# Down projections of a SwiGLU block: two 256-column products joined into one of 512 columns

## The reference, cut to what matters

```python
D_MODEL, SEQ, DEC_SEQ, D_FF = 1024, 512, 32, 2816
def swiglu(x, w_gu, w_down):
    gate, up = jnp.split(x @ w_gu, 2, axis=-1)
    return (jax.nn.silu(gate) * up) @ w_down

h = h + 0.5 * swiglu(rms_norm(h, p['norm_ffn1'][l]), p['ffn1_w_gu'][l], p['ffn1_w_down'][l])
```

## Time and profile before

| | us |
|---|---|
| median of 3 runs | 2352.0 |
| lowest, highest | 2350.32, 2352.34 |
| the profiled execution, its own time | 2351.26 |
| its span, first to last instruction | 2349.6 |
| PE busy | 2300.7 |
| DVE busy | 1721.3 |
| ACT busy | 1138.6 |

### The profile page before, as it was taken

The page is one execution under the profiler, slowest core; times in us unless marked ns, Lnnn a source line. Parts: engine busy times, 40 slices in busy tenths (PEclk is TensorE's granted clock), DMA queues, the critical chain, the costliest instruction groups (busy, mean ns, idle before and its releaser), DMA issues.

```text
span 2349.6 us, 49786 instructions
## 1 busy us (share of the span) xinstructions
PE 2300.7 (98%) x20579; PEld 2264.5 (96%) x20579; DVE 1721.3 (73%) x2569; ACT 1138.6 (48%) x1743; POOL 13.3 (1%) x50
## 2 busy tenths in 40 slices
PE   8999999999999999999999999999999999999998
PEld 8999999998999999999999999999999989999997
DVE  7767876788577567686867767876888867767875
ACT  6434444576355445343435434444677755434442
POOL 1000000000000000000000000000000000000000
PEclk9999999999999999999999999999999999999999
DMA  4333333332422233333333333332222223323331
GB/s 147 85 95 101 91 97 86 93 118 74 120 71 70 68 90 90 91 97 102 91 87 93 90 90 102 91 97 82 73 75 61 67 73 94 95 83 101 97 91 57
DMA packets 397772, 209.91 MB, mean 89 GB/s; under 512 B 11679, under 2 KB 393750, under 8 KB 397558
## 3 DMA queue, kind: packets, MB, share of 16 engines
q1 hardware_dynamic: 392166, 203.17, 30.4%
q10 hardware_dynamic: 5392, 3.72, 0.5%
HBM read 201.41 MB, written 5.45 MB: 88 GB/s over the span
## 4 chain that ended last, share of the span: by engine, by line
PE 71%; DVE 12%; ACT 6%; DVEq 6%; issue 3%; ACTq 1%; DMA 0%; SPq 0%
PE PM L2501 7%; PE PM L2503 7%; PE PM L2502 7%; PE PD L2417 7%; PE PD L2422 6%; PE PD L2423 6%; PE PD L2421 6%; PE PD L2418 6%; PE PD L2424 6%; PE PD L2503 3%; PE PD L2501 3%; PE PD L2502 3%; DVE wlo L1426 2%; ACT whi L619 1%; DVEq L1572 1%
## 5 line engine op out<-in xcount | busy, mean ns | idle before, releaser
L619 ACT ACTIVATE whi<-raw 128x1024 fp32r<-128x1024 f32 (+3 forms) x236 | 234.3, 993 | 362.4 <-PE PD L2424 356.4
L1426 DVE TENSOR_TENSOR wlo<-raw,whi 128x1024 fp32r<-128x1024 f32 (+3 forms) x238 | 273.5, 1149 | 87.1 <-ACT whi L619 65.3
L2417 PE MATMUL PD<-XB,whi 128*128 128x288 f32 x856 | 262.4, 307 | 4.8 <-DVE wlo L1426 4.5
L2422 PE MATMUL PD<-XB,whi 128*128 128x288 f32 x856 | 252.2, 295 | 0.0
L2423 PE MATMUL PD<-XB,wlo 128*128 128x288 f32 x856 | 252.0, 294 | 0.0
L2421 PE MATMUL PD<-XB,whi 128*128 128x256 f32 x856 | 241.2, 282 | 0.3 <-DVE XB L1464 0.3
L2418 PE MATMUL PD<-XB,whi 128*128 128x256 f32 x856 | 239.7, 280 | 0.0
L2424 PE MATMUL PD<-XB,wlo 128*128 128x256 f32 x856 | 237.5, 278 | 0.0
L2417 PE MATMUL PD<-AB,whi 128*128 128x288 f32 x704 | 209.8, 298 | 5.6 <-ACT AB L722 4.6
L2501 PE MATMUL PM<-XT,WH 128*128 128x272 f32 x720 | 208.3, 289 | 4.7 <-ACT PM L698 3.3
L2503 PE MATMUL PM<-XT,WL 128*128 128x272 f32 x720 | 208.2, 289 | 0.0
(11 more groups left out here) (500 smaller groups left out, 6590.1 us busy)
## 6 DMA issues: line engine op xcount, KB each, us to landing
raw<-in_ffn_w_down SPq DMA_DIRECT2D x64, 512.0 KB, 3.8
V<-in_ffn_w_gu SPq DMA_DIRECT2D x60, 512.0 KB, 4.0
V<-in_ffn_w_gu SPq DMA_DIRECT2D x120, 256.0 KB, 4.5
raw<-in_ab_w_in SPq DMA_DIRECT2D x44, 512.0 KB, 3.9
raw<-in_ffn_w_gu SPq DMA_DIRECT2D x32, 512.0 KB, 3.9
raw<-in_c_w_in SPq DMA_DIRECT2D x32, 512.0 KB, 4.1
raw<-in_ffn_w_down SPq DMA_DIRECT2D x32, 384.0 KB, 3.3
VF<-in_ffn_w_gu SPq DMA_DIRECT2D x12, 512.0 KB, 4.8
```

Source lines behind the costliest of these rows:

```text
L619: A(whi[ps % 2][:, 0:k, :], raw[ps % 4][:, 0:k, :], ACT.Copy).then_inc(S["hi_ready"], 1)
L1426: TT(wlo[u % 2][:, 0:k, :], raw[u % 4][:, 0:k, :], whi[u % 2][:, 0:k, :].bitcast(F), ALU.subtract).then_inc(S["lo_ready"], 1)
L2417: mm(front, hi, x[:, 0, r, 0:FRONT], start=first, stop=False)
L2422: mm(front, hi, x[:, 1, r, 0:FRONT], start=False, stop=False)
```

## The change

For a unit of a block's first two groups (`joined`, 64 units), the two products of the high weights by the rear tokens, one with high and one with low x, become one matmul of 512 columns: the moving operand is a view of both halves of x, and the result fills the whole rear bank (`rests`), sum of high in the first 256 columns and of low in the next. The other four matmuls are as they were; the one with the low weights adds to the first 256 columns. The wait for the low part of x stands ahead of the merged matmul. When the unit is read, DVE multiplies the second 256 columns into the scratch tile UR, before the line is released, and adds them to H in a second step. Units of the third group and all other units are unchanged.

```diff
+        def rests(b):
+
+            at0 = 1024 * (b % 2) + 512
+            return PDF[:, at0:at0 + 2 * REST].rearrange("p (s t) -> p s t", s=2)
+
+        def joined(u):
+
+            return any(plan[f"{tag}_down{g}"][0] <= u < plan[f"{tag}_down{g}"][0] + KT for tag, _ in FFNS for g in range(len(GROUPS) - 1))
...
             def scaled_residual(m, ps):
 
                 TT(RT[:, :], line(ps), RS[:, :], ALU.mult)
+                if joined(ps):
+                    TT(UR[:, 0:REST], rests(ps)[:, 1, :], RS[:, FRONT:T], ALU.mult)
                 dve.drain().then_inc(S["pair_read"], 1)
                 STT(H[:, m, :], RT[:, :], 0.5, H[:, m, :], ALU.mult, ALU.add)
                 dve.drain()
+                if joined(ps):
+                    STT(H[:, m, FRONT:T], UR[:, 0:REST], 0.5, H[:, m, FRONT:T], ALU.mult, ALU.add)
+                    dve.drain()
...
                 mm(front, hi, x[:, 0, r, 0:FRONT], start=first, stop=False)
-                mm(rest, hi, x[:, 0, r, FRONT:T], start=first, stop=False)
-                if before:
-                    before(1)
-                mm(rest, hi, x[:, 1, r, FRONT:T], start=False, stop=False)
+                if joined(ps):
+                    if before:
+                        before(1)
+                    mm(rests(ps), hi, x[:, :, r, FRONT:T], start=first, stop=False)
+                else:
+                    mm(rest, hi, x[:, 0, r, FRONT:T], start=first, stop=False)
+                    if before:
+                        before(1)
+                    mm(rest, hi, x[:, 1, r, FRONT:T], start=False, stop=False)
```

## The result

The changed kernel takes 2365.48 us in the median (2362.57 to 2365.91, 5 runs) against 2352.0 before: a ratio of 1.0052, 95% interval 1.0037 to 1.0067. Slower by 13.5 us between the medians (12.2 by the ratio), where 4 were forecast and 2361.5 was the upper end. The profiled execution took 2365.91, its span is 2364.2.

A forecast was written before the change was run, and what follows sets the result against it. PE was taken as the bound, with DVE close behind. Six-row groups +5.8, their late exit +1.0, eight-row groups -2.6 and first rows -0.2 gave +4.0 us: 2356.0, 0.17% slower, range 2350.0 to 2361.5.

The forecast's parts named there:

- The merged matmul, 0.225 us: PE, joined rows: 512 columns take 0.225 us start to start against the pair's 0.236, gaining 0.0116 us a row.
- the gain of 2.6 in eight-row groups: PE, eight-row groups: seven units of each group count, saving 2.6 us over the four FFNs.
- the two paces: PE: rows run at 0.747 or 0.753 us without a nameable cause, scattering the forecast by 2 us.
- proportional 512: Rival, chance 0.22: merged matmul on PE costs 0.236 or more, saving nothing; +7.7 us, 2359.7.
- cheap 512: Rival, chance 0.13: merged matmul on PE takes 0.215, saving 0.021 a row; +1.3 us, 2353.3.
- The merged wait, taken at 0: PE, group's last hidden row: waiting for x's low part hides under the existing bubble; 0, upper bound 0.9 us.
- DVE's added time, 0.84: DVE, each joined unit: product 0.34 plus second addition 0.50, together 0.84 us, 54 us over all.
- The chain: DVE, six-row groups: late reads delay the low weights, so PE waits at units 5, 6 and 7.
- the recurrence: Step-by-step DVE read times in the six-row group from unit 2: group longer by 1.54 us, later FFNs +1.37.
- the dear matmul: Merged matmul at 0.236 instead of 0.225: six-row group +1.75 a FFN, exit 0.18.
- The exit, 0.25 behind the group's end: After each six-row group: line 1548 on DVE comes 0.25 late and PE pays it, +1.0 us in all.
- The eight-row groups hide it: DVE, eight-row groups: 1.17 us idle less 0.84 and 0.09 leaves 0.2, so the added work is hidden.

The follow-up runs named there:

- dve_only: Kernel before, six matmuls a row, with only DVE's two added 256-column operations in the 64 units: 2361.47 us, ratio 1.0039.
- filled_joined: Changed kernel with unread 272-column matmuls put into PE's wait at each group's last hidden row: 2360.46 us, ratio 1.0041 to the kernel before.
- early_next_joined: Changed kernel with the next down unit's first rows put ahead of the group's last hidden row on PE: 2355.01 us, ratio 1.0018 to the kernel before.
- second_only: Kernel before with the change in the six-row groups alone (32 units): 2360.61 us, ratio 1.0047.
- first_only: Kernel before with the change in the eight-row groups alone (32 units): 2351.84 us, ratio 1.0000.

## Why the prediction was wrong, by its steps

*The merged matmul, 0.225 us.* This step failed: the term was sized too small. I had two readings of the excess over the columns' own time, fixed per matmul or growing with them, and took the fixed one for the reason that both rows near by showed "about that excess". The rows spoke for the other: 0.016 for 32 columns where 0.013 are the columns. Measured 0.234 in place, 0.232 in a plain stream. Of the gain of 2.6 in eight-row groups nothing came, but for the 0.4 that stems from the two paces. The rival "proportional 512" was the case: +7.7, 3.7 more than the forecast's sum; "cheap 512", 0.215, was not.

*The merged wait, taken at 0.* This step failed too, and its upper bound held: 0.10 for each of eight groups. The bubble behind the wait was not covered by the longer matmul but added to it: 0.34 to the next start, where the matmul takes 0.234 without a wait.

*DVE's added time, 0.84.* Right: 0.82. *The chain* was right in its mechanism: PE's starts of units 5, 6 and 7 from that of unit 2 were computed at 13.43, 18.47 and 23.97, and are 13.48, 18.49 and 23.97 in the first block (units of 4.49, 4.49, 4.50, 5.01, 5.48). At unit 5 the match is a coincidence: the forecast had it wait for 0.2 behind units of 4.41, and it does not wait, since three units of 4.49 take as long; units 6 and 7 wait as computed. From the start of unit 1 to the end of unit 7 the group takes 33.06 us where it took 31.36, so it lost 1.70, where the recurrence gave 1.54, or 1.75 with the dear matmul.

*The exit, 0.25 behind the group's end.* With the dear matmul it was computed at 0.18. It cost 0.13 in the first and 0.12 in the fourth block, and 0.47 and 0.48 in the middle two. There DVE stands idle once for a part that the profile puts down to nothing but "issue", 0.49 ahead of line 1524 in the third block (0.14 in the others), and in the second:

```profile
1125.12 1.76 DVE L1551 TENSOR_TENSOR WL<-V,WH 128x1536 fp32r<-128x1536 f32 x1 [0.43 <-issue]
```

The same two idle times stand in dve_only, filled_joined and early_next_joined, and not in second_only, whose six-row groups have the same edit. Why is open.

*The eight-row groups hide it.* Right for these groups by themselves, shown by first_only.

*What the sum did not hold* is the clock. No step asked what PE's pause at the last hidden row does to it; it stood at nothing without a reason, and the scatter that I allowed was for the two paces of the rows. Three falls cost 4.6 us in the profiled execution. That the pause has a part in them is supported by filled_joined and early_next_joined; why the merged form tips it and the six-matmul form, whose pause is 0.1 us shorter, does not, is open.

With the dear matmul and the wait the terms are 7.7 + 0.8 = 8.5, which gives 2360.5, still inside the range. The clock's 4.6 makes it 13.1, against 13.5 between the medians. That this comes so near is partly luck, for 4.6 is the price of one execution. The five executions differ: two with a mean granted clock of 0.997 took 2362.57 and 2363.07, three with 0.995 or 0.996 took 2365.48 to 2365.91. So the lower mean clock goes with 2.4 to 3.3 us, and at 0.997 the loss is still 10.6 to 11.1, where the table has 5.8 + 1.6 + 0.8 = 8.2 outside the clock and the scatter. The 2 to 3 us that remain are open, like the 2 of dve_only.

## What to carry to other kernels

Before two matmuls are merged, read from the rows how start-to-start time grows with width: here the excess grew with the columns, the wider matmul saved next to nothing, and what was added on the engine beside it was most of the effect. Follow a full neighbour engine step by step: the same 0.84 us was free at 1.17 us of idle, and 0.34 was free even where idle was zero, because slack further on absorbed it. And where an engine waits for a chain through two others, look for work of the next unit that can go there.

## What the runs showed of the hardware

One-pass float32 matmuls on this kernel's operands take, start to start at 2.4 GHz, 0.118 us for 256 columns and 0.232 for 512, but 0.111 for 192 and 0.110 for 128. That the weight loads set the pace there is likely and not shown: they are busy all the time in those stretches (2.66 of 2.66 and 2.65 of 2.65), but so they are at 256 and 320 columns, where the time still follows the columns. After a wait the next start is 0.10 to 0.11 later than without one: 0.23 instead of 0.12 at 256 columns, 0.24 instead of 0.13 at 288 (253.57 to 253.81 in the changed kernel), 0.34 instead of 0.234 at 512. Two-operand DVE operations ran at 1.04 ns a column and about 0.15 us (0.41 for 256 columns, 0.72 for 544, 1.76 for 1536).
